# Decode attention: the scores of the chosen rows on VectorE, one row to a partition, in place of turned keys and matmuls

## What is computed

```python
def nsa_cmp_slc(q, rows, qpos, cmp_w1, cmp_w2, cmp_pe, blocked):
    kc = compress(rows[:, :, 0], cmp_w1[0], cmp_w2[0], cmp_pe[0])
    vc = compress(rows[:, :, 1], cmp_w1[1], cmp_w2[1], cmp_pe[1])
    o_cmp, p = cmp_attention(q, kc, vc, qpos)
    kb = to_blocks(rows[:, :, 2])
    vb = to_blocks(rows[:, :, 3])
    sel = select_blocks(p, qpos, kb.shape[2])
    ...
def selected_attention(q, kb, vb, sel, qpos):
    kg = kb[bi, hi, sel]
    vg = vb[bi, hi, sel]
    s = jnp.einsum('bqhgd,bqhkld->bqhgkl', q, kg) * NSA_DH ** -0.5
    ...
    p = masked_softmax(s, mask, (-2, -1))
    return jnp.einsum('bqhgkl,bqhkld->bqhgd', p, vg)
```

## Time and profile before

| | |
|---|---|
| median of 3 runs | 2218.85 us (2215.81 to 2220.64) |
| the profiled execution | 2220.69 us |
| its span on the core | 2218.8 us |
| TensorE's mean granted clock | 0.982 |
| TensorE busy | 2144.7 us (97%) |
| VectorE, ScalarE, GpSimd busy | 904.0, 574.7, 645.3 us |
| decode and output phase | about 1213 us to the end |

### The profile page before, as it was taken

How to read it: one execution, slowest core, us unless ns; L and a number is a source line. 1 busy time by engine, 2 the same in 40 slices (tenths; PEclk the granted TensorE clock), 3 DMA queues, 4 the chain that set the end, 5 groups by cost and what they waited for, 6 DMA issues and landing times. The chain is left out here.

```text
span 2218.8 us, 25408 instructions
## 1 busy us (share of the span) xinstructions
PE 2144.7 (97%) x9871; PEld 1436.4 (65%) x9871; DVE 904.0 (41%) x1873; ACT 574.7 (26%) x1067; POOL 645.3 (29%) x682
## 2 busy tenths in 40 slices
PE   8999999999989999999997999999999999999997
PEld 7888888888878887777774555544555444434442
DVE  0453545455430014444444344544545444331227
ACT  0231133213300003233233333333333333210013
POOL 0000000000010003333337437666666666233000
PEclk9999999999999999999998999999999999999999
DMA  5212221222131221111113535456464666435114
GB/s 189 94 57 77 77 77 57 77 77 77 58 106 57 89 88 54 39 58 39 39 39 102 165 92 169 136 176 190 135 197 132 182 189 212 177 143 176 77 76 153
DMA packets 66387, 244.14 MB, mean 110 GB/s; under 512 B 10948, under 2 KB 28496, under 8 KB 53872
## 3 DMA queue, kind: packets, MB, share of 16 engines
q1 hardware_dynamic: 34040, 136.44, 17.5%
q0 software_dynamic: 32256, 106.46, 16.2%
HBM read 222.26 MB, written 20.59 MB: 109 GB/s over the span
## 5 line engine op out<-in xcount | busy, mean ns | idle before, releaser
L283 PE MATMUL pj<-xT,strips 128*128 128x260 f32 x2304 | 525.5, 388 | 8.6 <-DMA xT<-d_xT 8.6
L1488 PE MATMUL dpH<-XT,w 128*128 128x512 f32 x1024 | 516.9, 612 | 1.0 <-DVE XT L1693 0.7
L283 PEld LDWEIGHTS pj<-xT,strips 128*128 128x128 f32 x2304 | 438.5, 193 | 80.4 <-issue 14.6
L758 PE MATMUL mpj<-xT,strips 128*128 128x260 f32 x1280 | 313.8, 390 | 6.8 <-ACTq L962 5.7
L1435 POOL DMA_INDIRECT KV<-d_cache,gi x256 | 244.1, 954 | 261.6 <-PE dtb L1589 152.8
L1693 DVE COPY XT<-dtb 64x512 f32<-64x512 f32 x256 | 174.9, 683 | 280.7 <-PE dtb L1465 278.9
L758 PEld LDWEIGHTS mpj<-xT,strips 128*128 128x128 f32 x1280 | 233.1, 191 | 65.4 <-issue 27.5
L1694 ACT ACTIVATE XT<-dtb 64x512 f32<-64x512 f32 x256 | 152.7, 596 | 431.3 <-PE dtb L1465 430.6
L1488 PEld LDWEIGHTS dpH<-XT,w 128*128 128x128 f32 x1024 | 168.1, 192 | 125.5 <-issue 121.9
L988 POOL COPY PT<-old 64x256 f32<-64x256 f32 x16 | 9.8, 610 | 655.5 <-ACTq L962 654.6
L1001 POOL TENSOR_SCALAR old<-old,rd 128x128 f32<-128x128 f32 (+3 forms) x128 | 137.3, 1084 | 187.4 <-DVE rd L1102 187.1
(11 more groups left out here) (299 smaller groups left out, 2242.2 us busy)
## 6 DMA issues: line engine op xcount, KB each, us to landing
strips<-d_w_in SPq DMA_DIRECT2D x61, 1024.0 KB, 4.9
xT<-d_w_out SPq DMA_DIRECT2D x4, 4096.0 KB, 13.2
d_win_sample<-Wt SPq DMA_DIRECT2D x8, 1024.0 KB, 6.4
Xr<-d_w_out SPq DMA_DIRECT2D x2, 4096.0 KB, 14.4
Wt<-d_win SPq DMA_DIRECT2D x8, 896.0 KB
xT<-d_xT SPq DMA_DIRECT2D x4, 1040.0 KB, 11.3
Sold<-d_state SPq DMA_DIRECT2D x8, 512.0 KB, 5.7
d_hgrn_sample<-Snew SPq DMA_DIRECT2D x8, 512.0 KB, 4.1
```

Of the source, the lines that this page charges most:

```text
L283: mm = nc.tensor.matmul(pj[b][:, a, 0:TH], w[b][:, k, :], xT[:, k, a * TH:(a + 1) * TH], start=(k == 0), stop=(k == KT - 1))
L758: mm = nc.tensor.matmul(bank(s)[:, n, 0:TH], w[s % 2][:, k, :], xT[:, k, n * TH:(n + 1) * TH], start=(k == 0), stop=(k == KT - 1))
L1488: mm = nc.tensor.matmul(pH[g % 2][:], w1[:, g % 2, n, :], XT[g % 2][:, jp, :, r:r + HSUB], start=(n == 0), stop=(n == NS - 1))
```

## The change

The keys of the chosen rows are no longer turned. Instead the queries are brought to every partition. At the start of the phase TensorE turns all queries, VectorE orders them into `qrow`, SyncE writes them to `q_rows` in device memory, and before each sample it reads that sample's 1024 numbers back to all 128 partitions (`qB`, 0.5 MB). Each quarter has four pieces (two tiles by two pairs of heads), all on VectorE: a product of the keys in `KV` with `qB` into the second bank of `pS` (`prod`, 128x512) and a sum over the 64 columns of a head into `st` (one row to a partition, 8 scores). A sample has 16 such pairs, in a chain by `pr_r` and `kq`. SCORES, now at (1,10), turns `st` by eight transposes into `pS` and adds the newest key's column by two matmuls. GpSimd's `chosen` waits for `kq` of the quarter before instead of for the transposes. `KwT` has a buffer of its own, and `st` is cleared at the start. The pieces of the quarters stand at new places, and SCORES to VALUES two steps or more later.

```diff
-        KgT = sb("KgT", [P, 2, NT * P])
-        KwT = KgT[:, :, WIN:2 * WIN]
+        KwT = sb("KwT", [P, 2, WIN])
+
+        qB, st = sb("qB", [P, 2, 2 * G, DH]), sb("st", [P, NT, RS])
...
+        prod = pS[:, 512:1024].rearrange("p (a d) -> p a d", d=DH)
+        qrow = qB[0:NB].rearrange("p a g d -> p (a g d)")
...
-            (2, 4): "keys0", (2, 6): "keys0odd", (3, 4): "keys1", (3, 6): "keys1odd",
-            (0, 4): "KEYS2", (0, 6): "KEYS2ODD", (1, 4): "KEYS3", (1, 6): "KEYS3ODD",
-            (1, 8): "SCORES", (1, 10): "SCALE", (1, 12): "TURNED", (1, 15): "VALUES",
+            (2, 4): "keys0a", (2, 6): "keys0b", (2, 8): "keys0c", (2, 10): "keys0d",
+            (3, 4): "keys1a", (3, 6): "keys1b", (3, 9): "keys1c", (3, 11): "keys1d",
+            (0, 4): "KEYS2A", (0, 6): "KEYS2B", (0, 7): "KEYS2C", (0, 9): "KEYS2D",
+            (1, 4): "KEYS3A", (1, 6): "KEYS3B", (1, 8): "KEYS3C", (1, 9): "KEYS3D",
+            (1, 10): "SCORES", (1, 12): "SCALE", (1, 14): "TURNED", (2, 1): "VALUES",
...
-            (0, 2, 8): "keys0", (0, 2, 10): "keys0odd", (0, 3, 14): "keys1", (1, 0, 0): "keys1odd",
-            (1, 1, 4): "KEYS2", (1, 1, 6): "KEYS2ODD", (1, 2, 10): "KEYS3", (1, 2, 12): "KEYS3ODD",
-            (1, 2, 14): "SCORES", (1, 3, 0): "SCALE", (1, 3, 2): "TURNED", (1, 3, 5): "VALUES",
-            (1, 3, 6): "NEWEST0", (1, 3, 8): "NEWEST1", (1, 3, 10): "WSCORES",
-            (1, 3, 12): "WSCALE", (1, 3, 14): "WTURNED", (2, 0, 1): "WVALUES", (2, 0, 3): "SUM", (2, 0, 8): "DONE",
+            (0, 2, 8): "keys0a", (0, 2, 10): "keys0b", (0, 2, 12): "keys0c", (0, 2, 14): "keys0d",
+            (0, 3, 14): "keys1a", (1, 0, 0): "keys1b", (1, 0, 2): "keys1c", (1, 0, 4): "keys1d",
+            (1, 1, 4): "KEYS2A", (1, 1, 6): "KEYS2B", (1, 1, 8): "KEYS2C", (1, 1, 10): "KEYS2D",
+            (1, 2, 10): "KEYS3A", (1, 2, 12): "KEYS3B", (1, 2, 13): "KEYS3C", (1, 2, 14): "KEYS3D",
+            (1, 3, 0): "SCORES", (1, 3, 2): "SCALE", (1, 3, 4): "TURNED", (1, 3, 7): "VALUES",
+            (1, 3, 8): "NEWEST0", (1, 3, 10): "NEWEST1", (1, 3, 12): "WSCORES",
+            (1, 3, 14): "WSCALE", (2, 0, 0): "WTURNED", (2, 0, 2): "WVALUES", (2, 0, 4): "SUM", (2, 0, 9): "DONE",
...
+            def queries(b):
+                need(sp, kq, 16 * b)
+                sp.dma_start(qB[:].rearrange("p a g d -> p (a g d)"),
+                             io["q_rows"][b:b + 1].to_broadcast([P, KVH * G * DH])).then_inc(qb_in, 16)
+
+            sp.wait_ge(qr_r, 1)
+            sp.dma_start(io["q_rows"], qrow).then_inc(qr_out, 16)
+            sp.wait_ge(qr_out, 16)
             for b in range(NB - 2):
+                queries(b)
...
-                    for key in QUARTERS[q - 1]:
-                        bank, k = place[key, b if q else b - 1]
-                        pool.wait_ge(tr[bank], k + 1)
                     pool.wait_ge(v_r, 4 * b + q)
+                    pool.wait_ge(kq, 16 * b + 4 * q)
...
+                pe.wait_ge(kq, 16 * b + 16)
                 need(pe, e_w, b)
-                scores_of(b, pS, KgT, 512)
-                scores_of(b, pS, KgT, NSLC - 512, 512).then_inc(ss, 1)
+                for t in range(NT):
+                    n = P if t < NT - 1 else SL
+                    nc.tensor.transpose(pS[0:RS, t * P:t * P + n], st[0:n, t, :], ident[0:n, 0:n])
+
+                for hp in range(2):
+                    mm = nc.tensor.matmul(pS[32 * hp:32 * hp + 2 * G, NSLC - 1:NSLC], qbd[b % 2][:, hp, :],
+                                          keep["ksS"][:, hp, b:b + 1], start=True, stop=True)
+                mm.then_inc(ss, 1)
...
+            for n in range(2 * KVH):
+                mm = nc.tensor.transpose(pS[0:NB, n * P:(n + 1) * P], qS[:, n, :], ident)
+            mm.then_inc(qr_t, 1)
...
+            def keys(q, i):
+
+
+                t, hp = 2 * q + i // 2, i % 2
+                n = P if t < NT - 1 else SL
                 def do(b):
-                    v.wait_ge(g_in, 512 * b + 128 * (q + 1))
-                    need(v, pv_s, b)
-                    if q < 3:
-                        V.tensor_copy(Vg[:, 2 * q:2 * q + 2], KV[:, :, :, RUN - DH:RUN]).then_inc(v_r, 1)
-                    else:
-                        V.tensor_copy(Vg[:, NT - 2], KV[:, 0, :, RUN - DH:RUN])
-                        V.tensor_copy(Vg[0:SL, NT - 1], KV[0:SL, 1, :, RUN - DH:RUN]).then_inc(v_r, 1)
-                        need(v, sw, b)
-                        V.tensor_copy(KgT[:, :, NSLC - 1:NSLC], keep["ksS"][:, :, b:b + 1]).then_inc(kn_r, 1)
-                    empty_quarter(b)
+                    if i == 0:
+                        v.wait_ge(g_in, 512 * b + 128 * (q + 1))
+                        need(v, pv_s, b)
+                        if q < 3:
+                            V.tensor_copy(Vg[:, 2 * q:2 * q + 2], KV[:, :, :, RUN - DH:RUN]).then_inc(v_r, 1)
+                        else:
+                            V.tensor_copy(Vg[:, NT - 2], KV[:, 0, :, RUN - DH:RUN])
+                            V.tensor_copy(Vg[0:SL, NT - 1], KV[0:SL, 1, :, RUN - DH:RUN]).then_inc(v_r, 1)
+                        if q == 0:
+                            v.wait_ge(qb_in, 16 * b + 16)
+                            need(v, ss, b)
+                            need(v, e_s, b)
+                    k = 16 * b + 4 * q + i
+                    need(v, kq, k)
+                    V.tensor_tensor(prod[0:n].rearrange("p (a g) d -> p a g d", a=2),
+                                    KV[0:n, t % 2, 2 * hp:2 * hp + 2, 0:DH].unsqueeze(2).to_broadcast([n, 2, G, DH]),
+                                    qB[0:n, hp].rearrange("p (a g) d -> p a g d", a=2), ALU.mult).then_inc(pr_r, 1)
+                    v.wait_ge(pr_r, k + 1)
+                    V.tensor_reduce(st[0:n, t, 32 * hp:32 * hp + 2 * G], prod[0:n], AX_X, ALU.add).then_inc(kq, 1)
```

More of the change, by code:

```diff
@@ L1236, in decode_output_phase @@
         yq = Vg[0:NB].rearrange("p t h d -> p (t h d)").rearrange("p (q n) -> p q n", q=NQ4)
-        ys = KgT[0:NB, 0, 0:512]
+        ys = KwT[0:NB, 0, 0:512]
         flat = hs2[:].rearrange("p a h n -> p (a h n)")
@@ L1246, in decode_output_phase @@
         w_in, w_out, new_in = sem("w_in"), sem("w_out"), sem("new_in")
-        g_in, v_r, kn_r = sem("g_in"), sem("v_r"), sem("kn_r")
+        g_in, v_r, pr_r, kq = sem("g_in"), sem("v_r"), sem("pr_r"), sem("kq")
+        qr_t, qr_r, qr_out, qb_in = sem("qr_t"), sem("qr_r"), sem("qr_out"), sem("qb_in")
         tr, ev = [sem("tr0"), sem("tr1")], [sem("ev0"), sem("ev1")]
@@ L1311, in put @@
             counts[bank] += n
-        QUARTERS = ("keys0", "keys0odd"), ("keys1", "keys1odd"), ("KEYS2", "KEYS2ODD"), ("KEYS3", "KEYS3ODD")
-        TURNS = ("turned", *sum(QUARTERS, ()), "NEWEST0", "NEWEST1", "TURNED", "WTURNED", "DONE")
+        QUARTERS = ["keys0" + c for c in "abcd"], ["keys1" + c for c in "abcd"], ["KEYS2" + c for c in "ABCD"], [
+            "KEYS3" + c for c in "ABCD"]
+        TURNS = ("turned", "NEWEST0", "NEWEST1", "TURNED", "WTURNED", "DONE")
         for u in range(8):
@@ L1372, in _ @@
             weights(0)
+            queries(NB - 2)
             window(NB - 2)
@@ L1380, in _ @@
             sp.dma_start(gb, io["ln"].unsqueeze(0).to_broadcast([P, 2, D])).then_inc(gb_in, 16)
+            queries(NB - 1)
             window(NB - 1)
@@ L1408, in _ @@
             nc.gpsimd.memset(pn[:], 0.0).then_inc(init, 1)
+            nc.gpsimd.memset(st[:], 0.0).then_inc(init, 1)
             nc.gpsimd.memset(sc[:], FORCED).then_inc(init, 1)
@@ L1577, in rows @@
                 mm.then_inc(ix, 1)
[L1579 to L1593, removed]
             def turned_in(key):
@@ L1599, in chosen_scores @@
             def chosen_scores(b):
-                for key in QUARTERS[3]:
-                    turned_in((key, b))
-                pe.wait_ge(kn_r, b + 1)
+                pe.wait_ge(kq, 16 * b + 16)
                 need(pe, e_w, b)
-                scores_of(b, pS, KgT, 512)
-                scores_of(b, pS, KgT, NSLC - 512, 512).then_inc(ss, 1)
+                for t in range(NT):
[5 more added lines that the diff above has]
+                mm.then_inc(ss, 1)
             def newest(b, hp):
@@ L1672, in _ @@
                 "turned": turned, "sums": sums, "values": values, "rows": rows,
-                **{QUARTERS[q][par]: keys(q, par) for q in range(4) for par in range(2)}, "SCORES": chosen_scores, "NEWEST0": lambda b: newest(b, 0),
+                "SCORES": chosen_scores, "NEWEST0": lambda b: newest(b, 0),
                 "NEWEST1": lambda b: newest(b, 1), "WSCORES": newest_scores, "TURNED": chosen_turned,
@@ L1713, in empty_keys @@
                 eng.wait_ge(*free_of)
-            src = tb[bank][:, 0:m] if m == WIN else tb[bank][0:DH].rearrange("p (a n) -> p a n", a=2)[:, :, 0:m]
+            src = tb[bank][:, 0:m]
             if bank == 0:
@@ L1720, in key_pieces @@
         def key_pieces(eng):
[L1722 to L1725, removed]
             def newest(hp):
```

(16 more changed lines are left out.)

1 line of the change is left out of this document (removed).

## The result

The changed kernel takes 2317.6 us (median, 2307.4 to 2319.6), the kernel before 2219.7 beside it: 1.043 times as long, 95% interval 1.039 to 1.047. The forecast was 2329. On another chip the same pair gave 1.041 (1.038 to 1.044). The profiled execution has a span of 2317.4 us, 98.6 more than before.

A forecast was written before the change was run, and what follows sets the result against it. It took a ring of page gathers on GpSimd's queue, together with TensorE, as the bound. 7 + 82 + 6 + 15 = 110 us on the profiled 2220.7 gave 2331, 2329 as a median; range 2283 to 2373.

The forecast's parts named there:

- the ring: Four legs through GpSimd's gathers and the waits around them, closing once a pass: 109.4 us instead of 93.1.
- first K1: First start of GpSimd's quarter-1 gather block: D grows by 7.5 less 1.7, A by 0.8; +7 us.
- five rings: From product 8 of group 3 in pass 1 to that of pass 6, 109.4 us against 93.1: +82.
- the tail: Last two samples among output products: waits for VectorE against less TensorE work; net +15 us, bounds -5 and 35.
- A: Leg from the start of GpSimd's quarter-1 gather block to product 8 of group 3: 25.7 us, before 24.9.
- B: Leg from product 8 of group 3 to the start of GpSimd's quarter-3 gather block: 28.1 us, before 21.4.
- C: Leg from the start of GpSimd's quarter-3 gather block to product 8 of group 1: 25.1 us, before 23.8.
- D: Leg from product 8 of group 1 to the start of GpSimd's quarter-1 gather block: 30.5 us, before 23.0.
- GpSimd's delay: Gathers slowed beside VectorE's new products, about two in each of A and C: 0.4 us each, bounds 0 and 0.7.
- (a): Rival: pages come early enough through unseen slack, so TensorE's gain counts; 38 us won, 2181 us; chance 4%.
- (b): Rival: only places move, VectorE keeps up; B and D grow 5.5 each, +60 to +75, 2285 us; chance 13%.
- (c): Rival: VectorE falls further behind, rows land after 8 us, products cost GpSimd 0.7; +150, 2369 us; chance 16%.

The follow-up runs named there:

- Pages first: Each GpSimd block gathers pages before chosen rows: changed kernel 2221.8 us, 1.001 of the kernel before; same edit in the kernel before 2185.6 us, 0.986.
- the split wait: Changed kernel, first four gathers of a quarter wait only for the second pair of the quarter before: 2244.0 us, 0.971 of the changed kernel.
- the places: Kernel before with last key transposes and SCORES to VALUES at the changed kernel's places, nothing new on VectorE: 2511.8 us, 1.030 on the slower chip.
- load alone: Kernel before plus sixteen unused product-and-sum pairs a sample on VectorE, on constants: 1.001 on the slower chip, 1.008 on a usual one.
- the last variant: Changed kernel with pages before chosen rows, the wait split, and SCORES, SCALE and TURNED one step later: 2168.3 us, 0.978 of the kernel before.

## Why the prediction was right, point by point

**The direction and the cause** are as forecast: two waits for page gathers a pass, 8.2 to 9.9 us at (3,8) (forecast 9) and 6.4 to 6.5 at (1,8), 9.8 in pass 7 (forecast 8), a pass of 108.7 us (forecast 109.4), released by the fourth pairs. Pages first and the split wait move the time as the ring says, and so do the places on the slower chip; load alone does not.

**The sum** against the span's 98.6: first K1, 5.8 (1372.42 instead of 1366.64 at (3,8) of pass 1), forecast 7; five rings 79, forecast 82; to (1,8) of pass 7, 9, forecast 6; the tail 5, forecast 15. So 98.6 came where 110 was added up, and the tail is the term that was mis-sized. Its three waits for VectorE (rows as above):

```profile
2048.12 0.54 PE L1571 MATMUL dtb<-const,pn 40*128 40x40 f32 x2 [12.20 <-DVE pn L1845]
2069.31 1.11 PE L1607 MATMUL dpS<-const,st 128*40 128x128 f32 x8 [1.80 <-DVE st L1931]
2154.82 1.11 PE L1607 MATMUL dpS<-const,st 128*40 128x128 f32 x8 [2.76 <-DVE st L1931]
```

They were put at 16, 6 and 7 us; 12.2, 1.8 and 2.8 came. The chain has the last gathers of three quarters before the first two of them, from issue to landing:

```profile
2014.55 4.11 DMA KV<-d_cache,gi
...
2035.11 7.44 DMA KV<-d_cache,gi
...
2060.37 2.69 DMA KV<-d_cache,gi
```

X, the fourth pair of quarter 0, ends at 2005.04. TensorE wanted the weights at X+30.9, as forecast (31); they were ready at X+43, not X+47. Most of that is an error of adding: I took eight gathers at 1.25 and then 5 or 9 us for the last, but a landing in the earlier trace rows runs from the start of the last gather's issue, so it comes on top of seven, and the row says 8.06. From quarter 1's end (2025.60) to K2's rows (2042.55) it was 17.0 us, not 19.5.

**The legs** agree less well than their sum. With the starts above: A 22.7 to 23.3 (forecast 25.7), B 29.9 (28.1), C 23.7 (25.1), D 32.4 (30.5). A and C were too long by the landing: 3.8 and 3.6 us, where I had taken 6.0 and 5.4 from the kernel before. Why it is shorter in the changed kernel no run shows. B and D were too short, and there a step of mine failed, which is also told wrongly ahead of the prediction: it is not so that VectorE empties bank 0 and ScalarE bank 1. Both empty every turned piece, VectorE the lower 64 partitions (256 copies of 64x512 in a span, one for each of 256 turns). So in leg D three copies stand between the pairs, not one, and in leg B the fourth pair of quarter 1 also waits for the turn of (3,10). VectorE in order of time behind (3,8):

```profile
1589.98 0.68 DVE L1703 COPY XT<-dtb 64x512 f32<-64x512 f32 x1 [7.34 <-PE dtb L1484]
1590.64 0.75 DVE L1990 TENSOR_TENSOR oT<-dtb,ngS 64x4 f32<-64x4 f32 x4
1591.54 0.70 DVE L1927 TENSOR_TENSOR dpS<-KV,qB 128x512 f32<-128x512 f32 x1
1592.27 0.69 DVE L1931 TENSOR_REDUCE st<-dpS 128x8 f32<-128x512 f32 x1
1594.26 0.68 DVE L1703 COPY XT<-dtb 64x512 f32<-64x512 f32 x1 [1.30 <-PE dtb L1484]
1594.87 0.68 DVE L1927 TENSOR_TENSOR dpS<-KV,qB 128x512 f32<-128x512 f32 x1
1595.59 0.69 DVE L1931 TENSOR_REDUCE st<-dpS 128x8 f32<-128x512 f32 x1
```

K2 starts 8.2 us after (3,8), not 4.3: the last product of an older sample (L1990), which I had left out, then the wait for a turn, then its copy, and last the way to GpSimd. From the end of a fourth pair to the gather that it releases the trace has 0.8 us (1596.28 to 1597.06, 1674.04 to 1674.83); I had put 0.2 in legs D and B and nothing before K2. The error in B was covered in part by two that went the other way: K2's rows landed 3.0 us after the last gather's issue (1605.81 to 1608.85), and K3 hardly waited for VectorE. The fourth pair of quarter 2 ends at 1617.97, GpSimd's own last gather of K2 at 1618.01 (rows below): the two bound leg B together. That the sum of the legs came out within 1 us is luck in part.

**The prices** held, most of them: product 0.68 (forecast 0.69), sum 0.69 (0.68), eight transposes 1.13 at a mixed clock (0.87), the four one-column matmuls 0.13 (0.3), a wait of 2.6 us at (0,10) (2). TensorE's busy time was to fall by some 35 us less the low clock's share: it fell by 3.4, at a mean granted clock of 0.956 instead of 0.982. The 35 themselves show only with the waits gone: 2129.2 us in the kernel before with pages first, 2093.9 in the last variant.

**GpSimd's delay** by VectorE was put at 0.4 us for each new product. Block K2, in which four products fall, in the chain of work (start, us):

```profile
1609.57 1.36 POOL Xr L1438
1611.23 0.95 POOL Xr L1438
1612.48 0.99 POOL Xr L1438
1613.78 1.15 POOL Xr L1438
1615.23 0.95 POOL Xr L1438
1616.48 1.53 POOL Xr L1438
```

The products start at 1609.43, 1611.98, 1613.42 and 1616.55; the four gathers beside them take 0.41, 0.04, 0.20 and 0.58 us more than 0.95, 0.31 each. (The chain ends the last one at its release; in GpSimd's own list it takes 1.57.) The mean hides that most of them overlap a product only in part. The one at 1616.48 lies beside a whole product and loses about its length; but the one at 1635.06 in block K3, beside the whole product of 1635.04, takes 0.95 and loses nothing. The Trainium skill ("SBUF — State Buffer", section "SBUF: two separate sides") would have the one that starts later wait for the whole instruction of the other. The first gather, 0.54 us before the end of its product, loses 0.41, which is near that; the one at 1616.48, which started before its product, and the one at 1635.06 are not as it says. Whether the issue of a gather is an operation of the kind that the page means, no run here shows.

**The rivals.** (a) needed the pages early enough; no wait at (1,8) was its mark, and there were 6.4 us. (b), places alone, costs 3.0% by its own run, on the slower chip only; VectorE's pairs add to it on the usual one: halving them gives 3.5 us a pass. (c) asked for landings of 8 us; in the passes they were 3.6 to 3.9, and 7.6 only in pass 7. What stays open is how the 33 to 36 us that the changed kernel with pages first loses to the kernel before with pages first divide between the amount of VectorE's work and the chosen rows that are released late. Splitting the wait on top of pages first gained some 42 us, more than the deficit, so an earlier release can make up for it; no run separates the two shares.

## What to carry to other kernels

An engine that is 97% busy can share the bound with a queue; look for the wait that recurs once in every turn of a loop, and follow it back through the queue that feeds it until the loop closes. When a consumer moves to another engine or to a later place, the transfers that stand behind the wait for it move too: put the transfers that don't need that wait ahead of it, and make the wait as fine as the reads are. With the scores one step later besides, that turned a loss of 4% into a gain of 2%. Then give the old kernel the same queue before you judge the arithmetic: against it 0.8% is left.

## What the runs showed of the hardware that was not expected

The same kernel takes 2434 us on one chip and 2217 to 2221 on the others, at GpSimd's same pace of issue (a gather every 1.25 us). In the kernel with the unused pairs on the slower chip:

```profile
1667.36 0.96 POOL L1439 DMA_INDIRECT KV<-d_cache,gi  x1 [0.30 <-issue]
...
1670.98 0.60 PE L1469 MATMUL dtb<-const,xT 128*128 128x128 f32 x4
...
1681.26 0.68 DVE L1697 COPY XT<-dtb 64x512 f32<-64x512 f32 x1 [8.48 <-remote]
1682.09 1.03 PE L1593 MATMUL dtb<-const,KV 128*64 128x128 f32 x4 [7.46 <-DVE XT L1697]
```

From the last chosen-row gather of the block to the transposes that need it are 14.7 us, and I first took that for the gather's landing. But the transposes start right behind VectorE's copy of a turned piece (1681.26 to 1681.94), which empties the bank that they write; and that copy, of the turn at 1670.98, starts 10.3 us after its turn. On a usual chip the same copy follows its turn by 0.6 us (1564.18, 1564.82). ScalarE's copy of the same piece starts at 1681.26 too. Neither waits for a gather in the program, and the profile names their releaser "remote", one that it can't place. Copies of turned pieces with that releaser are in all four profiles of the slower chip (43 to 50 on VectorE, 198 to 239 us of waiting) and in none of the usual ones. What holds them no run shows. Pages first in the kernel before gained 2.7% there and 1.4% on the usual chip; the unused pairs cost nothing that can be told from zero there and 0.8% on the usual one. The places alone were run only there, so their share of the change's cost on the usual chips stays open.
